# Two transformer blocks: the last output branch and the second output projection with the second 128 tokens behind the first, the second norm through a diagonal, and the router by halves of the tokens

## The chip, the cores and the metric

The kernel runs on 1 core of one Trainium2 chip, in one launch. The metric is the device time in microseconds (us) of that core; three executions of the kernel before took 1136.58, 1136.77 and 1137.79 us.

## What is computed

256 tokens of width 1024 in f32 go through two blocks. The part that matters here is the end of the second block's mixer and the start of its expert stage:

```python
merged = jax.nn.sigmoid(gate_a) * (o_mla @ w_o_mla) + jax.nn.sigmoid(gate_b) * (o_fox @ w_o_fox)
x = x + gate_m * (merged @ w_out)
h = rms_norm_2(x, g_ffn_norm[l]) * (1.0 + scale_f) + shift_f
scores = jax.nn.sigmoid((xf @ w_router).astype(jnp.float32))     # xf is h, 256 x 1024; 64 experts
# top 4 of 8 groups, top 6 experts, gates; then per expert
hb = jax.nn.silu(xb @ w_exp_gate[e]) * (xb @ w_exp_up[e])
# ... @ w_exp_down[e], summed with the shared expert, and a last rms_norm
```

## The kernel before, in words

Every engine runs a list of instructions written out by hand, with semaphores between the lists. The tokens are two halves, m = 0 and m = 1, of 128 each.

**Projections.** A weight matrix comes in 1 MB loads into a ring of 6 slots (`ring`). A load is cut into "pieces" of two 128-row blocks of the contraction. ScalarE (ACT) writes a piece's rounded part into `hl` (6 places, `hi_of`), VectorE (DVE) writes the remainder into `rlo`, and TensorE (PE) does, for a piece and a half of the tokens, 6 matmuls of 512 columns into a PSUM bank. The activations are a pair in the same way: `L0` or `L1`, a rounded part by ACT (`rounded`) and a remainder by DVE (`completed`). `project` runs a block's pieces in steps. A step holds (piece s, m = 0) and (piece s - lag, m = 1); the table `BEHIND` names the blocks that share one run and their lag, all others have lag 0. A place in `hl` and a slot of `ring` are free only when both halves have used the piece (`both`), and the queue of SyncE (SP) waits for that before it issues the next load. Functions in `at` are called behind a step.

The blocks around the change, in order: `of0 of1` (the first output branch), `om0 om1` (the last, `w_o_mla`, 2 pieces each), `wp0 wp1` (the second output projection, `w_out`, 4 pieces each). Block x0 gives columns 0 to 511, x1 the others. Behind `om0` and `om1` DVE multiplies with the gate and adds (`branch`, semaphore `merged2`). `turn("mT2")` transposes the sum by 16 PE transposes in four groups; ACT and DVE make the pair in `L0`; `wp0` and `wp1` follow. Behind each of them DVE scales and adds to the residual `R` (semaphore `r2_set`), and ACT squares with a sum over the row (`sq2_a`).

**Second norm and router.** DVE and ACT make 1/root of each token; DVE scales m = 0 into `xp` and ACT m = 1; PE transposes `xp` (`turn("h3T")`, 16 transposes); DVE shifts and scales m = 0 into `ht3`, ACT m = 1. Then PE: router for both halves (16 matmuls of 64 columns, one bank, `taken` once), the shared expert's gate and up for m = 0 (16 matmuls of 256 columns), 16 transposes of `ht3` ("h3", banks 2, 3, 0, 1), gate for m = 1, the ranks (which need DVE's choice of experts, `sel_set`), up for m = 1, small transposes, and `gather(0)`, which starts the experts. A plain f32 matmul stands in the trace as two records.

**Experts.** 64 experts in 32 pairs, 3 MB of weights each, through 15 slots of 1 MB (`slots_all`). SP issues a load as soon as PE has used what was in the slot. Six slots are the ring's, some others hold buffers of the projections: nine loads wait for the end of `wp` or for what comes behind it.

**mod.** The modulation vector is summed on GpSimd; `mod_sum(11)` is the last PE step of it (a 512-column matmul of `macc` with ones), which stands between `wp0` and `wp1`.

## Time and profile before

| | |
|---|---|
| runs | 1136.58, 1136.77, 1137.79 us (median 1136.77) |
| profiled execution, its own time | 1138.23 us |
| its span | 1136.5 us, so 1.7 us lie around it |
| PE busy | 1066.9 us (94%) |
| last branch starts on PE | 553.14 us |
| second projection ends on PE | 594.64 us |
| first gather of the experts | 636.53 us |
| last write of a result | about 1136 us |

Times in rows are us from the span's start, durations of a group are for all its instructions, and "idle before" is how long the engine had nothing in work ahead of the row, with what released it. PEld is PE's loading of the stationary operand, which goes beside its matmuls. The granted clock is 1.00 at 2.4 GHz and 0.50 at 1.2 GHz.

### The profile page before, as it was taken

How to read it: one execution, taken by the hardware profiler on the slowest of the kernel's cores; microseconds unless marked ns; L12 is line 12 of the kernel's file. 1: busy time of each engine (PE TensorE's matmuls, PEld its weight loads, DVE VectorE, ACT ScalarE, POOL GpSimd, SP SyncE). 2: the span in 40 equal slices, each digit the busy share in tenths (PEclk: the TensorE clock that was granted, in tenths of full speed). 3: DMA queues.
4: the chain of work that ended last, by engine and by line, in shares of the span. 5: the costliest groups of instructions: out<-in, count | busy, mean ns of one | idle time of the engine just before them, and what ended most of it. 6: DMA issues, size and time to landing. Idle time of an engine off the chain costs nothing. (4 is left out here: it accounts for less than half of the span.)

```text
span 1136.5 us, 12858 instructions
## 1 busy us (share of the span) xinstructions
PE 1066.9 (94%) x5006; PEld 708.3 (62%) x5006; DVE 552.4 (49%) x985; ACT 392.5 (35%) x677; POOL 339.2 (30%) x261
## 2 busy tenths in 40 slices
PE   6999999979999899899797999999999999999993
PEld 4887888868887788688576645353535444444442
DVE  5979766758657766764744312222222221212214
ACT  4645665446424554564323101111211111111112
POOL 1059855596685007909700000000000000000000
PEclk9999999989999899799896999999999999999997
DMA  9656653856665545454439299999999999999991
GB/s 327 212 185 220 218 189 134 331 175 225 240 225 183 181 148 185 149 186 150 176 135 400 78 394 416 412 417 417 417 418 418 418 416 417 416 417 416 419 369 38
DMA packets 93933, 320.65 MB, mean 282 GB/s; under 512 B 6288, under 2 KB 7328, under 8 KB 76976
## 3 DMA queue, kind: packets, MB, share of 16 engines
q1 hardware_dynamic: 92832, 316.07, 72.7%
q0 software_dynamic: 752, 3.22, 0.8%
q8 instruction: 41, 0.67, 0.2%
q10 hardware_dynamic: 288, 0.52, 0.1%
q14 instruction: 20, 0.16, 0.0%
HBM read 318.74 MB, written 1.05 MB: 281 GB/s over the span
## 5 line engine op out<-in xcount | busy, mean ns | idle before, releaser
L802 PE MATMUL ps<-hl,L 128*128 128x512 f32 (+1 forms) x1216 | 388.7, 401 | 14.0 <-DVE rlo L1602 8.5
L802 PEld LDWEIGHTS ps<-hl,L 128*128 128x128 f32 x1216 | 231.7, 193 | 64.1 <-issue 15.8
L1602 DVE TENSOR_TENSOR rlo<-ring,hl 128x1024 fp32r<-128x1024 f32 (+1 forms) x154 | 211.5, 1393 | 112.9 <-ACT hl L1236 112.5
L802 PE MATMUL ps<-rlo,L 128*128 128x512 f32 (+1 forms) x608 | 241.5, 397 | 0.0
L802 PE MATMUL ps<-slots_all,xe 128*64 128x512 f32 (+1 forms) x1056 | 226.9, 582 | 0.8 <-DVE rt L2385 0.8
L1236 ACT ACTIVATE hl<-ring 128x1024 fp32r<-128x1024 f32 (+1 forms) x154 | 158.9, 1054 | 182.0 <-PE ps L802 75.2
L763 POOL TENSOR_SCALAR ring<-ring,st 128x512 f32<-128x512 f32 x84 | 176.1, 2097 | 0.0
L791 POOL CAST two<-ident 64x128 fp32r<-64x128 f32 x64 | 19.1, 298 | 488.6 <-PE ps L802 487.1
L802 PEld LDWEIGHTS ps<-slots_all,xe 128*64 128x64 f32 x1056 | 73.9, 137 | 131.7 <-issue 128.5
L802 PEld LDWEIGHTS ps<-rlo,L 128*128 128x128 f32 x608 | 117.1, 193 | 24.8
L765 POOL TENSOR_TENSOR macc<-macc,ring 128x512 f32<-128x512 f32 x84 | 116.7, 1390 | 7.0
L802 PE MATMUL ps<-slots_all,hh 128*64 128x512 f32 x512 | 116.2, 596 | 0.0
L1608 DVE SCALAR_TENSOR_TENSOR hh<-ps,gslot,hh 128x256 f32<-128x256 f32 x32 | 15.5, 483 | 190.9 <-ACT hh L1236 190.9
L1236 ACT ACTIVATE hh<-ps 128x256 f32<-128x256 f32 x64 | 24.7, 387 | 207.1 <-PE ps L802 196.4
L1236 ACT ACTIVATE yy<-ps 128x512 fp32r<-128x512 f32 x64 | 35.0, 595 | 171.0 <-PE ps L802 165.4
L761 POOL TENSOR_SCALAR macc<-ring,st 128x512 f32<-128x512 f32 x12 | 20.6, 1718 | 219.3 <-DMA ring<-in_w_mod 191.5
L802 PEld LDWEIGHTS ps<-slots_all,hh 128*64 128x64 f32 x512 | 37.3, 138 | 73.0 <-issue 66.3
L1602 DVE TENSOR_TENSOR yy<-ps,yy 128x512 fp32r<-128x512 f32 x64 | 41.3, 686 | 58.8 <-ACT yy L1236 58.8
L802 PE MATMUL ps<-yy,ppt 128*128 128x512 f32 x256 | 65.2, 397 | 3.5 <-DVE yy L1602 3.5
L802 PE MATMUL ps<-pp,h3hl 128*128 128x512 f32 x256 | 59.7, 390 | 1.0 <-DVE rgt L1602 1.0
L1605 DVE TENSOR_SCALAR ppt<-ps,cols 128x256 fp32r<-128x256 f32 x32 | 15.5, 483 | 88.6 <-PE ps L802 88.6
L802 PEld LDWEIGHTS ps<-yy,ppt 128*128 128x128 f32 x256 | 48.2, 189 | 15.0 <-DVE yy L1602 4.5
(213 smaller groups left out, 915.9 us busy)
## 6 DMA issues: line engine op xcount, KB each, us to landing
slots_all<-in_w_exp_gate SPq DMA_DIRECT2D x64, 1024.0 KB, 19.9
slots_all<-in_w_exp_up SPq DMA_DIRECT2D x64, 1024.0 KB, 15.9
slots_all<-in_w_exp_down SPq DMA_DIRECT2D x64, 1024.0 KB, 16.7
ring<-in_w_in SPq DMA_DIRECT2D x49, 1024.0 KB, 5.4
ring<-in_w_mod SPq DMA_DIRECT2D x24, 1024.0 KB, 6.2
ring<-in_w_out SPq DMA_DIRECT2D x8, 1024.0 KB, 5.2
ring<-in_w_ple_gate SPq DMA_DIRECT2D x4, 1024.0 KB, 5.1
ring<-in_w_branch_a SPq DMA_DIRECT2D x4, 1024.0 KB, 7.2
```

The source lines that it names most:

```text
L761: e.tensor_scalar(acc, v, s, None, ALU.mult).then_inc(mac, 1)
L763: e.tensor_scalar(v, v, s, None, ALU.mult).then_inc(mac, 1)
L765: e.tensor_tensor(acc, acc, v, ALU.add).then_inc(mac, 1)
L791: x = e.tensor_copy(two[s, i % 2, :].rearrange("p (e c) -> p e c", e=2), spread(ident[s, 64 * r + 2 * i:64 * r + 2 * i + 2], 64))
L802: return e.matmul(o, l, r, start=start, stop=stop)
L1236: return e.activation(o, i, f, **kw)
L1602: return e.tensor_tensor(o, a, b, op)
L1605: return e.tensor_scalar(o, a, s1, s2, op0, op1) if op1 is not None else e.tensor_scalar(o, a, s1, None, op0)
L1608: return e.scalar_tensor_tensor(out=o, in0=a, scalar=s, in1=b, op0=op0, op1=op1)
```

## The change

It does these things:

1. `om0 om1` become one run with lag 3 (4 pieces, 7 steps), `wp0 wp1` one with lag 4 (8 pieces, 12 steps). The transposes of the merged sum go by halves: m = 0 behind step 4 of the first run, m = 1 behind step 1 of the second. DVE's branch and residual steps and ACT's squares are placed by half and column.
2. The scaled copy `xp` is gone. DVE writes the token's 1/root into a diagonal (`DIAG2`), and PE multiplies `R` with it (`h3_turn`, 8 plain f32 matmuls of 128 columns for each half, whose stationary operand is read with a stride of 8 elements), which transposes and scales at once. DVE shifts the first four of eight blocks of both halves, ACT the last four.
3. `mod_sum(11)` stands behind the first half's diagonal matmuls.
4. The router's matmuls go by halves, with the second half's diagonal matmuls and a part of the shared expert between them; ACT loads the table of the sigmoid ahead of its shifts; banks are given by hand, those of "h3" being 4 to 7.

```diff
+        def DIAG2(m):
+            return B(4)[:, m, 0:128]
...
-        BEHIND = (("bb0 bb1", 4), ("wo0 wo1", 4), ("c0", 4),)
+        BEHIND = (("bb0 bb1", 4), ("wo0 wo1", 4), ("c0", 4), ("om0 om1", 3), ("wp0 wp1", 4))
...
-        SUM_AT = {}
+        SUM_AT = {11: "end"}
...
-        AFTER = {"v0": "qT", "za0": "kT", "gb1": "yaT", "ba0": "ybT", "om1": "mT2"}
+        AFTER = {"v0": "qT", "za0": "kT", "gb1": "yaT", "ba0": "ybT"}
...
-        aux_turn_x("h3T", "va")
-        aux_x("router", "a")
...
+        aux(("h3T", 0, 0), "v", 0), aux(("h3T", 0, 4), "a", 2)
+        for c in MOD_SUM["end"]:
+            aux(("mod", c), "v", 4)
+        aux(("h3T", 1, 0), "v", 1), aux(("h3T", 1, 4), "a", 3)
+        aux("router", "a", 0)
+        aux(("sh", 0), "v", 2)
+        for n, (j0, m) in enumerate((j0, m) for j0 in (0, 4) for m in range(2)):
+            aux(("h3", m, j0), "v", 4 + n)
...
-            for name in ("om0", "om1"):
-                project(name, L1, l_ready("omT"))
-            turn("mT2", lambda m, j: GB2[:, m, 128 * j:128 * j + 128],
-                 lambda m, j0: w.wait_ge(merged2, 2 * (j0 // 4) + m + 1))
-            for name in ("wp0", "wp1"):
-                project(name, L0, l_ready("mT2"))
-            for c in MOD_SUM.get("end", ()):
-                mod_sum(c)
-
-
-            w.wait_ge(*evacuated("wp1", 1))
-            for name in aux_names[aux_dense - 4:aux_dense]:
-                w.wait_ge(*read(name))
-
-            def xp_ready(m, j0):
-                w.wait_ge(*((xp_v, 1) if m == 0 else (xp_a, 1)))
-
-            turn("h3T", lambda m, j: xp[:, m, 128 * j:128 * j + 128], xp_ready)
-            wait_turned("h3T")
-            b = take("router")
-            w.wait_ge(*here2("router"))
+            def merged_turn2(m):
+                turn_tokens("mT2", m, lambda m, j: GB2[:, m, 128 * j:128 * j + 128],
+                            lambda m, j0: w.wait_ge(merged2, 2 * m + j0 // 4 + 1))
+
+            project("om0", L1, l_ready("omT"), {4: lambda: merged_turn2(0)})
+            project("wp0", L0, l_ready("mT2"), {1: lambda: merged_turn2(1)})
...
+            def h3_turn(m):
+                w.wait_ge(*evacuated("wp0", m))
+                w.wait_ge(*evacuated("wp1", m))
+                spread_tokens("h3T", m, lambda m, j: R[:, m, :].rearrange("p (f k) -> p k f", k=8)[:, j, :], DIAG2,
+                              lambda m, j0: w.wait_ge(xp_set, m + 1))
+
+            def route(b, m):
+                w.wait_ge(*here2("router"))
+                for k in range(8):
+                    wait_read(("h3T", m, 4 * (k // 4)))
+                    x = mm(b[:, 64 * m:64 * m + 64], ht3[:, k, tok(m)], wr[:, k, :], k == 0, k == 7)
+                return x
...
-            b = take(("sh", 0))
-            shared_half(b, 0, "sg", wsg, 0)
-            taken(shared_half(b, 0, "su", wsu, 256))
+            h3_turn(0)
+            for c in MOD_SUM["end"]:
+                mod_sum(c)
+            br = take("router")
+            route(br, 0)
+            h3_turn(1)
+            b0 = take(("sh", 0))
+            shared_half(b0, 0, "sg", wsg, 0)
+            taken(route(br, 1))
+            taken(shared_half(b0, 0, "su", wsu, 256))
...
+            project("om0", at={5: lambda: rounded("mT2", tokens=(0,))})
+
+            def square2(m, c):
+                w.wait_ge(r2_set, 2 * m + c + 1)
+                act(B(2)[:, m, half(c)], R[:, m, half(c)], ACT.Square,
+                    accum_out=st[:, 64 + 2 * m + c:65 + 2 * m + c]).then_inc(sq2_a, 1)
+
+            def square_root2(m):
                 w.wait_ge(rt2_v, m + 1)
                 act(st[:, 68 + m:69 + m], st[:, 68 + m:69 + m], ACT.Sqrt).then_inc(rt2_a, 1)
-            w.wait_ge(rt2_v, 3)
-            act(xp[:, 1, :].rearrange("p (k f) -> p f k", k=8), R[:, 1, :].rearrange("p (f k) -> p f k", k=8), ACT.Copy,
-                scale=st[:, 71:72]).then_inc(xp_a, 1)
-            w.wait_ge(xp_v, 1)
-            for j0 in (0, 4):
-                aux_done(("h3T", 1, j0))
-                for j in range(4):
-                    x = act(ht3[:, j0 + j, tok(1)], bank(("h3T", 1, j0))[:, 128 * j:128 * j + 128], ACT.Identity,
-                            scale=Af[:, j0 + j:j0 + j + 1], bias=modcol[:, 2, j0 + j:j0 + j + 1])
+
+            def h3_shift(m):
+                aux_done(("h3T", m, 4))
+                for j in range(4, 8):
+                    x = act(ht3[:, j, tok(m)], bank(("h3T", m, 4))[:, 128 * (j - 4):128 * (j - 4) + 128], ACT.Identity,
+                            scale=Af[:, j:j + 1], bias=modcol[:, 2, j:j + 1])
                 x.then_inc(aux_a.sem, 1)
+
+            def second_turned():
+                rounded("mT2", tokens=(1,))
+                act(st[:, 255:256], ones[:, 0:1], ACT.Sqrt)
+
+            project("wp0", at={2: second_turned, 3: lambda: square2(0, 0)})
+
+
+            square2(0, 1)
+            square_root2(0)
+            square2(1, 0)
+            square2(1, 1)
+            square_root2(1)
+            act(st[:, 255:256], ones[:, 0:1], ACT.Sigmoid)
+            h3_shift(0)
+            h3_shift(1)
...
+            project("om0", at={1: lambda: om(0, 0), 3: lambda: om(0, 1), 4: lambda: om(1, 0),
+                               5: lambda: completed("mT2", tokens=(0,))})
+            om(1, 1)
...
+            def diagonal2(m):
+                w.wait_ge(rt2_a, m + 1)
+                mine(e.reciprocal(st[:, 70 + m:71 + m], st[:, 68 + m:69 + m]))
+                wait_mine()
+                tsc(DIAG2(m), ident[:, :], st[:, 70 + m:71 + m], None, ALU.mult, None).then_inc(xp_set, 1)
...
-            root(0, rt2_v, rt2_a, mine)
-            wait_mine()
-            tsc(xp[:, 0, :].rearrange("p (k f) -> p f k", k=8), R[:, 0, :].rearrange("p (f k) -> p f k", k=8),
-                st[:, 70:71], None, ALU.mult, None).then_inc(xp_v, 1)
-            root(1, rt2_v, rt2_a, then3)
...
+            project("wp0", at={2: lambda: completed("mT2", tokens=(1,)), 3: lambda: wp(0, 0)})
+
+
+            wp(1, 0)
+            wp(0, 1)
+            w.wait_ge(sq2_a, 2)
+            mean_square(0, rt2_v)
+            diagonal2(0)
+            wp(1, 1)
+            h3_shift(0)
+            w.wait_ge(sq2_a, 4)
+            mean_square(1, rt2_v)
+            diagonal2(1)
+            for c in MOD_SUM["end"]:
                 mod_sum(c)
+            h3_shift(1)
...```

On PE, from the end of the second projection to the last transposes ahead of the gather (`bs` with `rbuf` is the diagonal with R). Before, then changed:

```order
L806 MATMUL ps0<-ident_49,xp_99 128x128 x4
L806 MATMUL ps1<-ident_49,xp_99 128x128 x4
L806 MATMUL ps2<-ident_49,xp_99 128x128 x4
L806 MATMUL ps3<-ident_49,xp_99 128x128 x4
L802 MATMUL ps0<-slots_all_97,ht3_85 128x64 x16
L802 MATMUL ps1<-slots_all_97,ht3_85 128x256 x16
L806 MATMUL ps2<-ident_49,ht3_85 128x128 x4
```

```order
L803 MATMUL ps0<-bs_70,rbuf_63 128x128 x4
L803 MATMUL ps2<-bs_70,rbuf_63 128x128 x4
L803 MATMUL ps4<-macc_79,ones_51 128x512
L803 MATMUL ps0<-slots_all_97,ht3_85 128x64 x8
L803 MATMUL ps1<-bs_70,rbuf_63 128x128 x4
L803 MATMUL ps3<-bs_70,rbuf_63 128x128 x4
L803 MATMUL ps2<-slots_all_97,ht3_85 128x256 x8
L803 MATMUL ps0<-slots_all_97,ht3_85 128x64 x8
L803 MATMUL ps2<-slots_all_97,ht3_85 128x256 x8
L807 MATMUL ps4<-ident_49,ht3_85 128x128 x4
```

The 16 router matmuls have become 8 and 8, and the second half's diagonal matmuls and 8 matmuls of the shared expert stand between them.

On DVE, through the run of `om0 om1` and the start of `wp0` (`ps0` to `ps3` are om0 m = 0, om0 m = 1, om1 m = 0, om1 m = 1; `rlo` is a weight piece's remainder, `L0` that of the transposed sum). Before, then changed:

```order
L1602 TENSOR_TENSOR bs_70<-ps1,bs_70 128x512
L1602 TENSOR_TENSOR bs_70<-bs_70 128x512
L1602 TENSOR_TENSOR rlo_67<-ring_65,hl_66 128x1024 x2
L1602 TENSOR_TENSOR bs_70<-ps2,bs_70 128x512
L1602 TENSOR_TENSOR bs_70<-bs_70 128x512
L1602 TENSOR_TENSOR bs_70<-ps3,bs_70 128x512
L1602 TENSOR_TENSOR bs_70<-bs_70 128x512
L1602 TENSOR_TENSOR L0_68<-ps6,L0_68 128x4x128
L1602 TENSOR_TENSOR L0_68<-ps7,L0_68 128x4x128
```

```order
L1615 TENSOR_TENSOR rlo_67<-ring_65,hl_66 128x1024
L1615 TENSOR_TENSOR bs_70<-ps1,bs_70 128x512
L1615 TENSOR_TENSOR bs_70<-bs_70 128x512
L1615 TENSOR_TENSOR rlo_67<-ring_65,hl_66 128x1024
L1615 TENSOR_TENSOR L0_68<-ps6,L0_68 128x4x128
L1615 TENSOR_TENSOR L0_68<-ps7,L0_68 128x4x128
L1615 TENSOR_TENSOR rlo_67<-ring_65,hl_66 128x1024
L1615 TENSOR_TENSOR bs_70<-ps3,bs_70 128x512
L1615 TENSOR_TENSOR bs_70<-bs_70 128x512
L1615 TENSOR_TENSOR rlo_67<-ring_65,hl_66 128x1024
L1615 TENSOR_TENSOR L0_68<-ps4,L0_68 128x4x128
L1615 TENSOR_TENSOR L0_68<-ps5,L0_68 128x4x128
```

The last branch step of the second half (`ps3`) now stands behind the remainders of the first half and behind one more weight piece, the fifth of `w_out`.

## Rows read from the trace of the kernel before

**Rows 1.** Waits of SP, 600 to 1100 us; its issues; the chain that ended last.

```profile
SPq L735 <- PE ps L802: 318.0, 57, 17.1
...
651.59 0.89 SPq L735 DMA_DIRECT2D slots_all<-in_w_exp_down  x2
...
1097.19 12.54 PE ps L802 x88
```

**Rows 2.** Timeline of PE, branch `om` and projection `wp`: start us, us.

```profile
553.14 1.04 PE L802 MATMUL ps<-hl,L 128*128 128x512 f32 x2
...
564.46 1.03 PE L806 MATMUL ps<-ident,bs 128*128 128x128 f32 x8
568.08 0.66 PE L806 MATMUL ps<-ident,bs 128*128 128x128 f32 x4 [2.59 <-DVE bs L1602]
...
570.10 1.05 PE L802 MATMUL ps<-hl,L 128*128 128x512 f32 x2
...
582.69 1.02 PE L802 MATMUL ps<-macc,ones 128*128 128x512 f32 x2
...
584.26 0.62 PE L802 MATMUL ps<-hl,L 128*128 128x512 f32 x2
...
593.80 0.62 PE L802 MATMUL ps<-hl,L 128*128 128x512 f32 x2
```

**Rows 3.** Stretches: start:end, length, busy us (instructions) by engine, PEclk, DMA share, GB/s.

```profile
570.00:575.00 5.00, 5.00 (x17) 3.89 (x16) 2.97 (x4) 3.26 (x5) 0.00 (x0) 0.66 0.01 5
```

**Rows 4.** ACT and DVE on weight pieces of `w_out`, and the page's DMA issues (last number: us to landing).

```profile
564.38 1.06 ACT L1236 ACTIVATE hl<-ring 128x1024 fp32r<-128x1024 f32 x1 [4.10 <-DMA ring<-in_w_out]
565.47 1.23 DVE L1602 TENSOR_TENSOR rlo<-ring,hl 128x1024 fp32r<-128x1024 f32 x1 [1.50 <-ACT hl L1236]
...
ring<-in_w_out SPq DMA_DIRECT2D x8, 1024.0 KB, 5.2
```

**Rows 5.** Timeline of DVE and ACT behind the projection.

```profile
594.68 0.69 DVE L1602 TENSOR_TENSOR bs<-ps,gbuf 128x512 f32<-128x512 f32 x1
596.26 0.63 ACT L1236 ACTIVATE bs<-rbuf 128x512 f32<-128x512 f32 x1 [0.77 <-DVE rbuf L1602]
600.40 1.37 DVE L1605 TENSOR_SCALAR ht<-ps,st,modcol 128x128 f32<-128x128 f32 x4 [0.63 <-PE ps L806]
603.11 3.15 ACT L1236 ACTIVATE ht<-ps,modcol,st 128x128 f32<-128x128 f32 x8 [1.27 <-PE ps L806]
606.28 1.28 ACT L1236 ACT_TABLE_LOAD   x1
```

**Rows 6.** Timeline from the router to the first gather, all engines.

```profile
606.67 16.21 PE L802 MATMUL ps<-slots_all,ht 128*128 128x64 f32 x64 [1.95 <-ACT ht L1236]
613.76 0.28 ACT L1236 ACTIVATE rt<-ps 128x128 f32<-128x128 f32 x1 [6.20 <-PE ps L802]
...
618.92 0.62 DVE L1602 TENSOR_TENSOR rt<-rt 128x128 f32<-128x128 f32 x2
...
622.72 1.91 PE L806 MATMUL ps<-ident,ht 128*128 128x128 f32 x16
...
625.33 3.72 PE L802 MATMUL ps<-slots_all,ht 128*128 128x256 f32 x16 [0.70 <-DVE h3hl L1602]
...
629.95 3.67 PE L802 MATMUL ps<-slots_all,ht 128*128 128x256 f32 x16
...
636.53 3.69 PE L802 MATMUL ps<-pp,h3hl 128*128 128x512 f32 x15 [1.05 <-DVE rgt L1602]
```

**Rows 7.** A stretch of the router, columns as in rows 3.

```profile
612.00:614.00 2.00, 2.00 (x10) 1.97 (x10) 0.00 (x0) 0.23 (x1) 0.00 (x0) 0.50 0.97 406
```

**Rows 8.** Weight loads and matmuls with small or strided operands: ns min/median/max, first and last start.

```profile
L802 PEld LDWEIGHTS ps<-bs,rbuf x16: 187/192/192, 385.2 to 386.8; 128*128 128x128 f32 x16
...
L802 PEld LDWEIGHTS ps<-ones,macc x16: 195/218/218, 343.0 to 344.7; 128*64 128x64 f32 x16
...
385.15 2.05 PE L802 MATMUL ps<-bs,rbuf 128*128 128x128 f32 x16 [0.59 <-DVE bs L1605]
```

More of the change, by code:

```diff
@@ L1174, in shared_down @@
             def shared_down():
-                wait_read(("sT", 0), ("sT", 1))
+                wait_turned("h3")
+                wait_read(("sT", 0), ("sT", 1), *aux_names[aux_dense - 4:aux_dense], *(("mod", c) for c in MOD_SUM["end"]))
                 w.wait_ge(*here2("sd"))
@@ L1505, in _ @@
             rounded("omT", (0,))
-            for name in ("om0", "om1"):
-                project(name)
-            rounded("mT2")
-            act(st[:, 255:256], ones[:, 0:1], ACT.Sqrt)
-            for c in range(2):
-                project(f"wp{c}")
-                for m in range(2):
-                    w.wait_ge(r2_set, 2 * c + m + 1)
-                    act(B(1)[:, m, half(c)], R[:, m, half(c)], ACT.Square,
-                        accum_out=st[:, 64 + 2 * m + c:65 + 2 * m + c]).then_inc(sq2_a, 1)
```

70 lines of the change are left out of this document (25 added, 45 removed).

## The prediction

> **What bounds the kernel now.** I read the page first: PE is busy for 94% of the span, so an idle or slow PE is what there is to win. The chain that ended last is PE almost alone from 671 to 1109.7 us [rows 1]: in the expert stage PE waits for no weights. SP there waits for PE, 318 us in 57 waits, since a slot is refilled when PE has used it, and the stream begins again at 651.6 with the first pair's slots [rows 1]. Both PE and the loads of this stage hang on the start of the first gather at 636.53 [rows 6]; what comes before moves the end of the kernel one to one, as long as the nine loads issued at the end of `wp` land first. So the question is how much earlier the gather starts.
>
> Ahead of it lie two stretches. **Stretch A** is 553.14 to 594.64, 41.5 us, from `om` to the end of `wp`. Between the two PE does 16 transposes and waits for DVE's last branch steps, from 564.46 to 570.10 [rows 2]. After that the granted clock is 0.66 over 5 us [rows 3], that is 3.4 us at 1.2 GHz. **Stretch B** is 594.64 to 636.53, 41.9 us: adds and squares, root, `xp`, transposes, shifts, and only at 606.67 the router [rows 5, 6], which runs at a granted clock of 0.50 [rows 7].
>
> **Stretch A, before.** Three matmuls of 512 columns take 0.68 us (14 triples from 584.26 to 593.80 [rows 2]), so a piece for half of the tokens takes 1.36. There are 24 of these: 32.6. The slow first ones cost 0.4, the turn 5.6, the slow clock behind it 1.7 (half of 3.4), `mod_sum(11)` 0.9 (two records and the slow one behind, 582.69 to 584.26 less 0.68 [rows 2]). Sum 41.2, measured 41.5.
>
> **Stretch A, changed.** The 32.6 and 0.4 stay. The transposes stay too, 8 in 1.03 us [rows 2], so 2.1, but other matmuls stand around them. The waits, counted from the start of `om` (t = 0):
> - m = 0 is done at 5.8, its branch step (0.69 + 0.69 [rows 5] and a gap, 1.4) at 7.3, its transposes start at 8.6, behind step 4: no wait. They end at 9.6, and PE does the last two pieces of m = 1 until 12.3.
> - DVE meanwhile does a piece's remainder (1.23 [rows 4]), `om0` m = 1, another remainder, then the first two remainders of L0. The third `w_out` piece needs step 4 (8.6), ACT 1.06, DVE 1.23, so L0's first group stands at 12.9. PE waits 0.6.
> - The fifth `w_out` piece is in a load that takes the slot of `om0`. Before, both halves had used `om0` after 4 piece-halves, now after 6, at 8.6. A load of `w_out` lands in 5.2 us [rows 4]; ACT before waited 4.10 us for this very one at 564.38 [rows 4]. So it lands at 13.9, is rounded at 15.0 and its remainder done at 16.2. The last branch step (`ps3`) is queued behind it on DVE: done at 17.6. PE has ended step 1 of `wp` at 15.7 and four of the transposes at 16.2, and waits 1.5 us.
> - The hl places of the seventh and eighth piece come free at steps 4 and 5 of the run; ACT and DVE need 2.5 us and each following step gives 2.7. Behind ACT's first square nothing is late. I cost this at nothing; if one of them slips by 1 us, PE waits 1 us.
>
> Sum 32.6 + 0.4 + 2.1 + 2.1 = 37.2 against 41.5: **4.3 us** earlier. Of these 0.9 are `mod_sum(11)`, which I count in B.
>
> **Stretch B, changed.** T is the end of `wp`. m = 0 is done 6.8 us ahead of T (five piece-halves), and its adds (1.4, and 1.4 of m = 1 between), square (0.63 [rows 5] and its sum), mean, root and diagonal take some 4.2. The diagonal is ready before T, hidden by matmuls of m = 1; without that cover it would cost those 4.2.
>
> The price of the diagonal matmuls is the open one. With R read in order, 16 records took 2.05 us [rows 8], 0.125 each; that is the lower end, 2.0 for a half. Here R is the stationary operand and is read with a stride of 8 elements. The one load with this stride takes 218 ns for 64 columns, where one in order takes 192 for 128 [rows 8]. If the excess goes with the columns, a record needs about 0.27 and a half of the tokens 4.3; that is the upper end. I take 4.3, since the strided row is the nearest one.
>
> The Trainium skill (SBUF — State Buffer, section "Door 1: The DMA port swizzle") says that f32 can be strided by up to four elements for free and that each access to a new 16-byte line pays. Eight elements are past that, so the rule speaks against this change and for the upper end: by it the gain of the next paragraph is 6.9, and if it did not hold it would be 9.8. No row shows a 128-column load with this stride.
>
> PE then: diagonal, half 0, 4.3; `mod_sum(11)` 1.0; router half 0, first four blocks, 1.0 (16 records at 0.125 are 2.0; DVE's shift, 1.37 [rows 5], is done at T + 3.6). The last four blocks wait for ACT. ACT's list is: last square (T + 2.4), root of m = 1 (its mean is behind DVE's shift, so T + 4.2), the table load of 1.28 [rows 5] and a dummy, T + 5.7, then four shifts (half of 3.15 [rows 5]), T + 7.3. PE waits 1.0. Then router 1.0; diagonal, half 1, 4.3; gate of m = 0 3.65 (8 matmuls, 3.72 and 3.67 [rows 6]); router half 1 2.0; up 3.65; 16 transposes 1.9 [rows 6]; gate of m = 1 3.65; ranks 1.0 (625.33 + 3.65 to 629.95 [rows 6]); up 3.65; and as before 2.9 from there to the gather (633.6 to 636.53). Sum 35.0. DVE's choice of experts takes 5.8 from the router (613.76 to 619.54 [rows 6]) and is hidden by 9.2 us of PE; the second half's shifts (1.6) by the gate's 3.65. Against 41.9: **6.9 us** earlier.
>
> The Trainium skill (ScalarE: Activation LUTs, section "What ACT_TABLE_LOAD costs") adds a drain of 1.38 us to each load, 2.66 in all. Here the load takes 1.28 and the rows do not show what came before it; with 2.66 the wait of 1.0 would be 2.4 and the gain 1.4 smaller.
>
> **The clock.** The sums hold at 2.4 GHz. In the trace it fell behind the turn of stretch A [rows 3] and in the wait of stretch B, where the router did not bring it back [rows 7]. In the changed kernel both places have less idle time, but B has 12 us of matmuls with few columns and a wait. I take one fall, at the price of stretch A's, 1.7 us. None would be 0; one in each stretch, the second through the gate of m = 0, 1.7 + 3.0.
>
> **Sum.** 4.3 + 6.9 - 1.7 = 9.5, so the profiled execution of 1138.23 becomes 1128.7. The median of the runs, 1136.77, is 1.5 below it, and becomes **1127.3 us**.
>
> **The rivals.**
> 1. *Stride costs nothing.* A half takes 2.0, so 4.6 less of PE work; the wait for ACT grows by 1.7 (its last shift then stands at T + 6.7, where PE is at T + 4.0), so 2.9 net. With no fall of the clock: 4.3 + 6.9 + 2.9 = 14.1, 1122.7. For it: the strided loads followed each other at 0.12 us (343.0 to 344.7 for 16 [rows 8]), like those in order. Against it: 218 ns for half the columns. Chance 0.22.
> 2. *Clock and waits take half.* Falls in both stretches (4.7) and 2 us more of waits where DVE has its 14 steps between 5 and 19 us of A: 11.2 - 6.7 = 4.5, 1132.3. For it: both places had a fall before [rows 3, 7]. Against it: PE's idle time in A falls from 3.3 (5.6 less 2.3 of transposes) to 2.1. Chance 0.20.
> 3. *Diagonal matmuls dearer than the whole gain.* The 32 strided records stand alone on PE from T on, twice. Slower than before needs 11.2 us more, 0.27 + 11.2/32 = 0.62 us a record; at 0.75 the time would be 1136.8 + 32 x 0.48 - 11.2 = 1141.0. For it: no row has this load. Against it: the 64-column one is at 0.22. Chance 0.06.
> 4. *The end does not follow the gather.* If the expert loads were the bound, an earlier PE would wait for them at the end, 1136.8. Against it: the loads resume when PE frees slots [rows 1], so they move too. It is also the case in which the change does not do what it says. Chance 0.04.
>
> **How the numbers follow.** The forecast has 0.48. Its own range is 1125.5 to 1130 (a fall of the clock or none, the table load). The range for 8 in 10 takes in rival 1 (down to 1121.8 with a part of the idle time of A gone as well) and rival 2 (1133.5 with 1 us more). A measurement of this kernel can tell about 0.2%, 2.3 us: faster than that are forecast, rivals 1 and 2, 0.90; rival 4 is the same, 0.04; rival 3 slower, 0.06.
>
> **What would show it.** In the changed profile: `om` to the end of `wp` in some 37 us, with a wait for DVE `bs` of about 1.5 ahead of four transposes; diagonal matmuls beginning within 0.3 us of the end of `wp`, 16 records in 4.3 us (2.0 for rival 1, over 9 for rival 3); a wait of about 1 us in the router for ACT `ht`; the gather at about 627; the expert stage as long as before, 473 us from the gather to 1109.7. The prediction is wrong if the gather comes after 634, or if it comes early and PE then waits for a load.

## The result, and the profile after

The changed kernel takes **1122.97 us** (median of four runs, 1121.79 to 1124.01), the kernel before beside it 1136.67 (four runs, 1136.20 to 1137.79): a ratio of 0.988, 95% interval 0.9867 to 0.9893. That is 13.7 us less; 9.5 were forecast (1127.3, range 1121.8 to 1133.5). The sign, the place and the order of the gains were right; the gain was 4.2 us larger than forecast.

The profiled execution took 1123.09 us, with a span of 1121.3. PE is busy for 95% of it. First the timeline of PE in stretch A (as in [rows 2]: start us, us):

```profile
551.03 1.05 PE L803 MATMUL ps<-hl,L 128*128 128x512 f32 x2
...
559.67 1.03 PE L807 MATMUL ps<-ident,bs 128*128 128x128 f32 x8
...
564.10 0.70 PE L803 MATMUL ps<-hl,L 128*128 128x512 f32 x2 [0.63 <-DVE L L1615]
...
566.95 0.60 PE L807 MATMUL ps<-ident,bs 128*128 128x128 f32 x4
568.61 0.66 PE L807 MATMUL ps<-ident,bs 128*128 128x128 f32 x4 [1.06 <-DVE bs L1615]
569.02 0.71 PE L803 MATMUL ps<-hl,L 128*128 128x512 f32 x2
...
588.08 0.40 PE L803 MATMUL ps<-rlo,L 128*128 128x512 f32 x1
```

(`ps` is PSUM, and `bs` a buffer that holds the merged sum and, later, the diagonal.) `om` begins at 551.03 and `wp` ends at 588.48 (588.08 and 0.40): 37.4 us, where [rows 2] had 41.5. The transposes, which stood in one block, are in two, with matmuls between them. Where [rows 3] had a granted clock of 0.66, it is now 1.00. Windows of PE only (stretch, length, busy us with its instructions, PEclk, DMA share, GB/s):

```profile
550.00:555.00 5.00, 5.00 (x20) 0.89 0.00 0
570.00:575.00 5.00, 5.00 (x23) 1.00 0.01 2
...
592.00:597.00 5.00, 3.75 (x23) 1.00 0.99 406
597.00:602.00 5.00, 5.00 (x23) 1.00 1.02 428
...
607.00:612.00 5.00, 5.00 (x33) 1.00 1.02 409
```

Stretch B, from 588.48 to the gather at 621.39, takes 32.9 us; before it took 41.9 [rows 5, 6]:

```profile
588.31 3.85 PE L803 MATMUL ps<-bs,rbuf 128*128 128x128 f32 x16
592.00 1.02 PE L803 MATMUL ps<-macc,ones 128*128 128x512 f32 x2
592.86 1.00 PE L803 MATMUL ps<-slots_all,ht 128*128 128x64 f32 x8
595.11 1.10 PE L803 MATMUL ps<-slots_all,ht 128*128 128x64 f32 x8 [1.25 <-ACT ht L1241]
596.05 4.02 PE L803 MATMUL ps<-bs,rbuf 128*128 128x128 f32 x16
599.91 8.86 PE L803 MATMUL ps<-slots_all,ht 128*128 128x256 f32 x48
608.61 1.91 PE L807 MATMUL ps<-ident,ht 128*128 128x128 f32 x16
...
621.39 7.55 PE L803 MATMUL ps<-pp,h3hl 128*128 128x512 f32 x32 [1.05 <-DVE rgt L1615]
```

The first diagonal matmul starts as `wp` ends: the norm of the first half is hidden. The router's first matmul comes 4.4 us behind the end of `wp`; before it came 12.0 behind ([rows 5] to [rows 6]). The router ran at a granted clock of 0.50 there [rows 7] and runs at 1.00 here. ScalarE shows what the wait of 1.25 is (answers to [rows 5]):

```profile
591.94 0.20 ACT L1241 ACTIVATE st<-st 128x1 f32<-128x1 f32 x1 [1.26 <-DVE st L1618]
592.16 1.28 ACT L1241 ACT_TABLE_LOAD   x1
593.46 0.20 ACT L1241 ACTIVATE st<-ones 128x1 f32<-128x1 f32 x1
593.57 1.49 ACT L1241 ACTIVATE ht<-ps,modcol,st 128x128 f32<-128x128 f32 x4
```

The shift that the router waits for stands behind the table load. In the expert stage nothing has changed but the time at which it starts. SP's issue and the chain that ended last, against [rows 1]:

```profile
636.46 0.89 SPq L736 DMA_DIRECT2D slots_all<-in_w_exp_down  x2
```

```profile
1082.04 12.54 PE ps L803 x88
```

Both are 15.1 us earlier, like the gather (636.53 to 621.39). Of these 15.1 us, 4.1 come from stretch A, 9.0 from B and 2.1 from ahead of `om`, which began at 553.14 before and at 551.03 now behind code that is the same. The unchanged kernels traced again, below, show that such shifts come and go.

### The profile page after: what moved, and what is told of

Read it like the earlier page. It is cut to its first block and busy times, and to the rows that moved or that the text cites. A ratio compares the mean times of both kernels' runs of the same rounds, so it can differ in the third digit from the quotient of the medians.

```text
span 1121.3 us, 12888 instructions
## 1 busy us (share of the span) xinstructions
PE 1059.9 (95%) x5022; PEld 705.2 (63%) x5022; DVE 546.5 (49%) x986; ACT 390.3 (35%) x677; POOL 338.4 (30%) x261
## 3 DMA queue, kind: packets, MB, share of 16 engines
HBM read 318.74 MB, written 1.05 MB: 285 GB/s over the span
## 5 line engine op out<-in xcount | busy, mean ns | idle before, releaser
L803 PE MATMUL ps<-hl,L 128*128 128x512 f32 (+1 forms) x1216 | 388.3, 401 | 14.4 <-DVE rlo L1615 8.5
L803 PEld LDWEIGHTS ps<-hl,L 128*128 128x128 f32 x1216 | 231.5, 193 | 63.7 <-issue 15.7
L1615 DVE TENSOR_TENSOR rlo<-ring,hl 128x1024 fp32r<-128x1024 f32 (+1 forms) x154 | 206.2, 1359 | 113.7 <-ACT hl L1241 113.3
L803 PE MATMUL ps<-rlo,L 128*128 128x512 f32 (+1 forms) x608 | 241.1, 396 | 0.0
L803 PE MATMUL ps<-slots_all,xe 128*64 128x512 f32 (+1 forms) x1056 | 226.9, 582 | 0.8 <-DVE rt L2406 0.8
L1241 ACT ACTIVATE hl<-ring 128x1024 fp32r<-128x1024 f32 (+1 forms) x154 | 158.8, 1055 | 182.5 <-PE ps L803 73.3
L764 POOL TENSOR_SCALAR ring<-ring,st 128x512 f32<-128x512 f32 x84 | 171.0, 2036 | 0.0
L803 PEld LDWEIGHTS ps<-slots_all,xe 128*64 128x64 f32 x1056 | 73.9, 137 | 131.7 <-issue 128.5
L803 PEld LDWEIGHTS ps<-rlo,L 128*128 128x128 f32 x608 | 117.1, 193 | 24.9
L766 POOL TENSOR_TENSOR macc<-macc,ring 128x512 f32<-128x512 f32 x84 | 120.1, 1430 | 7.0
L803 PE MATMUL ps<-slots_all,hh 128*64 128x512 f32 x512 | 115.7, 594 | 0.0
L1241 ACT ACTIVATE hh<-ps 128x256 f32<-128x256 f32 x64 | 24.7, 386 | 207.4 <-PE ps L803 196.7
L1241 ACT ACTIVATE yy<-ps 128x512 fp32r<-128x512 f32 x64 | 35.0, 595 | 170.7 <-PE ps L803 170.7
L803 PEld LDWEIGHTS ps<-slots_all,hh 128*64 128x64 f32 x512 | 37.2, 138 | 72.5 <-issue 65.9
L1615 DVE TENSOR_TENSOR yy<-ps,yy 128x512 fp32r<-128x512 f32 x64 | 41.3, 686 | 58.5 <-ACT yy L1241 58.5
L803 PE MATMUL ps<-yy,ppt 128*128 128x512 f32 x256 | 65.6, 399 | 3.5 <-DVE yy L1615 3.5
L803 PE MATMUL ps<-pp,h3hl 128*128 128x512 f32 x256 | 59.7, 390 | 1.1 <-DVE rgt L1615 1.1
L1618 DVE TENSOR_SCALAR ppt<-ps,cols 128x256 fp32r<-128x256 f32 x32 | 15.5, 484 | 88.6 <-PE ps L803 88.6
L803 PEld LDWEIGHTS ps<-yy,ppt 128*128 128x128 f32 x256 | 48.6, 191 | 15.1 <-DVE yy L1615 4.5
## 6 DMA issues: line engine op xcount, KB each, us to landing
slots_all<-in_w_exp_gate SPq DMA_DIRECT2D x64, 1024.0 KB, 19.8
slots_all<-in_w_exp_up SPq DMA_DIRECT2D x64, 1024.0 KB, 15.8
slots_all<-in_w_exp_down SPq DMA_DIRECT2D x64, 1024.0 KB, 16.6
ring<-in_w_in SPq DMA_DIRECT2D x49, 1024.0 KB, 5.5
ring<-in_w_mod SPq DMA_DIRECT2D x24, 1024.0 KB, 5.2
ring<-in_w_out SPq DMA_DIRECT2D x8, 1024.0 KB, 5.1
ring<-in_w_ple_gate SPq DMA_DIRECT2D x4, 1024.0 KB, 5.1
ring<-in_w_branch_a SPq DMA_DIRECT2D x4, 1024.0 KB, 6.6
```

Source lines behind the costliest of these rows:

```text
L764: e.tensor_scalar(v, v, s, None, ALU.mult).then_inc(mac, 1)
L766: e.tensor_tensor(acc, acc, v, ALU.add).then_inc(mac, 1)
L803: return e.matmul(o, l, r, start=start, stop=stop)
L1241: return e.activation(o, i, f, **kw)
L1615: return e.tensor_tensor(o, a, b, op)
L1618: return e.tensor_scalar(o, a, s1, s2, op0, op1) if op1 is not None else e.tensor_scalar(o, a, s1, None, op0)
```

## The experiments

A single kernel's runs spread by up to 6.7 us (`xp`), and the traced run need not be near the median: that of `first` was its slowest (1126.36), that of `p4` its fastest (1119.78). So single edits are read in the trace: by the length of A (start of `om` to end of `wp`), of B (to the gather), and of the rest (gather to the end of the span).

The column "before beside it" is the median of the kernel before, run in the same session.

| kernel | A | B | rest | median, us | before beside it | ratio, 95% interval |
|---|---|---|---|---|---|---|
| before | 41.5 | 41.9 | 500.0 | 1136.67 | | |
| before, again | 42.0 | 41.2 | 499.9 | 1136.58 | 1136.82 | 0.9997, 0.9987 to 1.0008 |
| changed | 37.4 | 32.9 | 499.9 | 1122.97 | 1136.67 | 0.988, 0.9867 to 0.9893 |
| changed, again | 38.9 | 33.2 | 498.4 | 1123.62 | 1136.82 | 0.9885, 0.9868 to 0.9901 |
| stride1 | 38.8 | 30.5 | 500.1 | 1123.98 | 1136.74 | 0.9887, 0.9875 to 0.99 |
| table | 38.8 | 31.6 | 501.6 | 1125.41 | 1136.74 | 0.9899, 0.9885 to 0.9914 |
| first | 43.3 | 31.5 | 498.4 | 1123.53 | 1136.74 | 0.9878, 0.9863 to 0.9892 |
| xp | 39.0 | 32.0 | 498.4 | 1125.64 | 1136.74 | 0.9899, 0.9883 to 0.9916 |
| uom | 43.6 | 32.9 | 500.0 | 1128.65 | 1135.74 | 0.9937, 0.992 to 0.9953 |
| uwp | 41.8 | 35.5 | 500.0 | 1130.71 | 1135.74 | 0.9967, 0.9953 to 0.9981 |
| warm (on before) | 42.0 | 35.6 | 501.6 | 1132.27 | 1135.74 | 0.9968, 0.9958 to 0.9978 |
| p4 | 36.2 | 33.2 | 498.3 | 1122.23 | 1135.74 | 0.9895, 0.9876 to 0.9913 |
| late_before (on before) | 37.9 | 41.5 | 500.0 | 1132.48 | 1137.88 | 0.9955, 0.9939 to 0.997 |
| mixed_p4 | 37.7 | 28.6 | 500.0 | 1120.76 | 1136.82 | 0.986, 0.9845 to 0.9876 |

**What varies by itself.** The two kernels were traced again.

> The changed kernel, unchanged, for a second trace. Theory, its terms that hang on waits and instruction counts come again (waits of 0.63 and 1.06 to 1.5 in the stretch of om and wp, 1.25 in the router, diagonal 3.7 and 3.9, last stretch 32.9), and what differs is where the clock is half: the start of om costs 1.3 more where it is, and the expert stage takes 498.4, 499.9 or 501.6 from the gather to the end, in steps of about 1.6. Median 1122 to 1124. Rival, the last stretch too has a fall of the clock in some executions, so 34 to 36.

> The kernel before, unchanged, for a second trace of it. Theory, the clock falls in the head of its last stretch in every execution, because TensorE idles there through the adds, squares, root and scaling: from the end of wp to the gather 41 to 42 us again, with the router at a granted clock of 0.50. The stretch of om and wp again has a fall behind its turn: 41 to 43. Rival, the fall at the router is one of those that come and go between executions, like the one at the start of om (absent in the changed kernel's first trace, there in four of its variants): last stretch 36 to 38.

The changed kernel's waits came again: 0.64 and 1.14 in A, 1.25 in the router. The start of `om` ran at a granted clock of 0.56 (550 to 555), which made A 1.5 longer. B had a small fall of the clock (0.88 and 0.78 over 595 to 605) worth 0.3. The rest differed by 1.5. In the kernel before, both falls came again (0.66 over 565 to 570, then 0.59, 0.50, 0.50, 0.70 from 595 to 615). So the low clock at the router belongs to that kernel, and the theory holds. The one at the start of `om` is no part of the change: the same kernel had it at 0.89 in one trace and at 0.56 in the other. In the second trace of the kernel before, `om` began at 548.88, 4.3 us earlier than in the first.

**Is the clock part of the gain?** In `warm` the kernel before got ten idle matmuls in stretch B, five of them behind `wp`, two and three around the transposes:

```
+            def warm(n):
+                for _ in range(n):
+                    mm(PS[7][:, :], ident[:, :], GATES[:, 0, half(0)], True, True)
...
+            warm(5)
```

> The kernel before, with ten idle f32 matmuls of 512 columns into an unused bank in the stretch behind wp: five after its last piece, two after the first four transposes and three after the last, where TensorE waits anyway. In the kernel before the granted clock was 0.50 from about 597.6 to 618.0. Theory, part of the gain of the change in this stretch (41.9 to 32.9, where 7 was forecast at full clock) is that the clock no longer falls: at half clock the 32 router matmuls took 7.05 instead of 4.0, the 16 of gate and up 9.0 instead of 7.3, the transposes 1.3 more. With TensorE kept busy the stretch takes 36 to 38 us instead of 41.9 and the time is 1131 to 1133. Rival, the low clock there costs nothing that counts, because VectorE's and ScalarE's steps set the pace, or the idle matmuls delay the real ones by as much as they save: stretch 41 to 43, time 1136 to 1138.

B fell from 41.9 and 41.2 to 35.6 (36 to 38 were expected), and the time by 3.5 us (in the trace 1.6 of it was given back behind the gather, rest 501.6). The router and what follows ran at full clock; the 64 matmuls of [rows 6] took 10.69 instead of 16.21 and 15.67:

```profile
602.90 2.74 PE L802 MATMUL ps<-gbuf,ident 128*128 128x512 f32 x6
605.47 10.69 PE L802 MATMUL ps<-slots_all,ht 128*128 128x64 f32 x64
```

The theory holds. About 6 of the 9 us that the change gains in B are the clock, which the idle head of B had pulled down and the small matmuls behind it had not brought back. Work of no use brings these 6 without any of the change. The rest, 35.6 to 32.9, is got by subtraction: it is what the lag, the diagonal and the router by halves bring together at full clock.

**The stride of the diagonal matmuls.** `stride1` reads R in order, which puts the features in another order and gives other values, with the same instructions:

```
-spread_tokens("h3T", m, lambda m, j: R[:, m, :].rearrange("p (f k) -> p k f", k=8)[:, j, :], DIAG2,
+spread_tokens("h3T", m, lambda m, j: R[:, m, 128 * j:128 * j + 128], DIAG2,
```

> The diagonal matmuls read 128 consecutive elements of R instead of every eighth (the features reach the expert stage in another order, so the values differ, but every instruction stays). Theory, the stride costs TensorE time: in the changed kernel a load of 128 columns with the stride took 313 to 336 ns and eight records with it 3.69 and 3.86 us, where loads in order take 192. Then eight records take about 2.0 us, TensorE's work falls by 1.7 to 1.85 per half, about 3.5 together. The first half's part is given back as a longer wait for ScalarE's half of the columns, since that is held up by the table load and the shift and not by TensorE; so the gather comes 1.8 to 2.2 us earlier and the time is 1120.9 (1120.6 to 1121.4). Rival, the 3.7 us is the price of f32 matmuls of 128 columns whatever the layout: eight records still take 3.7, loads over 300 ns, time 1123.0.

Weight loads of the changed kernel, then those of `stride1` (ns min/median/max, first and last start):

```profile
L803 PEld LDWEIGHTS ps<-bs,rbuf x32: 313/335/336, 588.1 to 599.5; 128*128 128x128 f32 x32
```

```profile
L803 PEld LDWEIGHTS ps<-bs,rbuf x32: 188/192/192, 590.6 to 599.7; 128*128 128x128 f32 x32
```

The 16 records take 1.78 us instead of 3.69: 0.11 each against 0.23. The stride doubles their spacing. As expected, the first half's saving went partly into the wait for ScalarE, 1.25 to 2.29, and B fell by 2.5 (1.8 to 2.2 were expected). The median does not show it (1123.98): A began at half clock, and 2.5 us is inside the spread of the runs. The mechanism is settled by the rows, not by the time.

**The wait in the router.** `table` leaves the small Sigmoid out; `first` puts the second diagonal ahead of the router:

```
-            act(st[:, 255:256], ones[:, 0:1], ACT.Sigmoid)
             h3_shift(0)
```

```
+            h3_turn(1)
             br = take("router")
             route(br, 0)
-            h3_turn(1)
```

> The small Sigmoid ahead of the first half's shift is left out, so the table load (1.28 us) is made by the router's Sigmoid instead. Theory, the wait of 1.25 us in the router matmuls for ScalarE's first half is the table load: that wait falls to 0.1 or nothing, the shift starts at the end of the first half's diagonal matmuls, and the load lies beside the second half's matmuls or the choice of experts, where ScalarE is ahead of TensorE: time 1121.8 (1121.5 to 1122.2). Rival, the load lengthens the chain from the router's scores through the choice of experts to the gather, which ends within 1.05 us of wait at the gather's start: what is gained ahead of the router is lost there, time 1123.0 or up to 0.3 more.

> The second half's diagonal matmuls stand ahead of the first half's router matmuls. Theory, TensorE's wait of 1.25 us for ScalarE's columns is filled by work that waits for nothing (the second half's diagonal was ready about 3.2 us before its use, at 592.7 against a start at 592.9, so 0 to 0.2 of it is waited for): time 1121.8 (1121.6 to 1122.2). Rival, the scores of the second half still come at the same place behind ScalarE's second shift, now waited for in turn, or the choice of experts is what the gather waits for, so the wait only moves: time 1122.8 to 1123.0.

PE in `table`, then in `first`:

```profile
594.61 2.00 PE L803 MATMUL ps<-slots_all,ht 128*128 128x64 f32 x16
596.45 4.02 PE L803 MATMUL ps<-bs,rbuf 128*128 128x128 f32 x16
```

```profile
572.12 1.12 PE L807 MATMUL ps<-ident,bs 128*128 128x128 f32 x4 [2.94 <-DVE bs L1615]
...
599.13 4.00 PE L803 MATMUL ps<-bs,rbuf 128*128 128x128 f32 x16
602.97 10.65 PE L803 MATMUL ps<-slots_all,ht 128*128 128x64 f32 x64
```

In both, the wait is gone and B is 1.4 shorter. `table` shows that the load was the wait, and both show that the choice of experts did not become the bound. In `table` the load runs at 602.03, in idle time of ScalarE. The medians say nothing of it. In the trace of `table` the gain came back behind the gather, where the clock fell (the 32 matmuls that start there took 9.15 us instead of 7.55): its rest is 1.7 longer. All four runs of `table` lie between 1125.1 and 1125.5, so this may belong to it; whether it does stays open. In `first`, A was 43.3 for another reason, which the row shows: a wait of 2.94 for DVE `bs`, to which the next point comes.

**The diagonal against the scaled copy.** `xp` scales R on VectorE into `xp` again, by halves, and transposes it.

```
-tsc(DIAG2(m), ident[:, :], st[:, 70 + m:71 + m], None, ALU.mult, None)
+tsc(xp[:, m, :].rearrange("p (k f) -> p f k", k=8), R[:, m, :].rearrange("p (f k) -> p f k", k=8),
+    st[:, 70 + m:71 + m], None, ALU.mult, None)
...
```

> The diagonal is undone: VectorE scales the half of R by the root's reciprocal into a copy with the features regrouped, as in the kernel before but by halves of the tokens, and TensorE turns that with eight transposes. Theory, the diagonal is the dear way: a scaling on VectorE takes 1.3 us instead of 0.29 for a diagonal, while eight transposes take about 2.0 (16 took 4.12 with the clock granted in full) against 3.69 and 3.86. First half: +1.0 on VectorE ahead of TensorE and -1.7 on TensorE, so -0.7, of which the wait for the table load gives back some; second half: the scaling is hidden behind TensorE and -1.8 remains. Time 1120.8 (1120.2 to 1121.8). Rival, the diagonal pays as built, because the scaling stands ahead of the transposes on the path in both halves (+1.0 and +1.0) and the shift behind them is what the router waits for: time 1123 to 1125.

```profile
589.15 1.03 PE L807 MATMUL ps<-ident,xp 128*128 128x128 f32 x8
590.02 1.02 PE L803 MATMUL ps<-macc,ones 128*128 128x512 f32 x2
592.10 1.10 PE L803 MATMUL ps<-slots_all,ht 128*128 128x64 f32 x8 [1.05 <-DVE ht L1618]
595.50 1.97 PE L803 MATMUL ps<-slots_all,ht 128*128 128x64 f32 x8 [2.29 <-ACT ht L1241]
597.26 1.92 PE L807 MATMUL ps<-ident,xp 128*128 128x128 f32 x8
```

B is 32.0, 0.9 less than with the diagonal and not the 2.2 of the theory. The first half's transposes are 2.8 us shorter, and the waits behind them 2.1 longer. Behind these the clock fell again (0.88, 0.50 and 0.94 in the three stretches of 5 us from 590): eight router records took 1.97 instead of 1.10, and the second eight transposes 1.92 instead of 1.03. For the first half, with the lists of DVE and ACT as they stand, the dear diagonal is thus nearly free, since PE would wait in its place; for the second half, where PE waits for nothing, it costs its whole price, which `mixed_p4` shows below. The median, 1125.64, is over what this trace gives; its six runs lie at 1121.2 to 1121.4 (two, the traced one among them) and 1125.5 to 1127.9 (four). Why, is open.

**What the lags bring.** `uom` takes the lag from `om` alone, `uwp` from `wp` alone. Of each, the entry in the table of runs; the turns, squares and branch steps then follow by blocks of columns:

```
-        BEHIND = (("bb0 bb1", 4), ("wo0 wo1", 4), ("c0", 4), ("om0 om1", 3), ("wp0 wp1", 4))
+        BEHIND = (("bb0 bb1", 4), ("wo0 wo1", 4), ("c0", 4), ("wp0 wp1", 4))
```

> The lag is taken out of the last output branch alone: each piece of om0 and om1 is again multiplied for both halves of the tokens at once, and the first half is turned when the branch has ended; the second projection keeps its lag. Theory, the lag of this run hides VectorE's branch steps behind the other half's matmuls: without it TensorE waits again after the last piece, 3.5 us in the kernel before (5.6 from 564.46 to 570.10 less 2.1 of transposes) against 0.63 and 1.06 in the changed kernel, so the stretch from om to the end of wp is 1 to 2 us longer (38.8 was measured where the clock is half at its start, so 39.8 to 40.8), and 1.7 more if the clock falls behind the wait. The stretch from there to the gather stays at 32.9. Time 1124.5 to 1126.5. Rival, the waits of this stretch come from the late w_out piece and its load and not from the order of the halves: the stretch keeps its length within 0.5 us, time 1123 to 1124.

> The lag is taken out of the second output projection alone: both halves of the tokens end within 0.7 us of each other, so the first half's adds, squares, root and diagonal have no matmuls of the second half to hide them. Theory, the cover is worth what lies between a half's last matmul and its diagonal, 4.2 us: TensorE waits 4 to 5 us between the end of wp and the first diagonal matmul, and the stretch from the end of wp to the gather grows from 32.9 to 37 or 38; if the clock falls in that wait and the small matmuls behind it don't bring it back, up to 3 more. The stretch of om and wp changes by -0.5 to +1.5 (the second half is turned ahead of wp instead of one step into it). Time 1127 to 1131. Rival, most of the gain in this stretch is the diagonal and the router by halves, not the lag: growth under 2 us, time 1123 to 1125.

In `uom`, A is 43.6, more than the 39.8 to 40.8 expected (42.5 with a fall of the clock) and than the 41.5 before: waits of 2.93 and 1.19, and a fall of the clock (0.75 and 0.57 from 565 to 575). In `uwp`, A is 41.8 and B 35.5:

```profile
568.41 1.09 PE L806 MATMUL ps<-ident,bs 128*128 128x128 f32 x4 [5.04 <-DVE bs L1617]
...
594.30 4.15 PE L802 MATMUL ps<-bs,rbuf 128*128 128x128 f32 x16 [2.13 <-DVE bs L1620]
```

The cover of the first half's norm is worth 2.1, half of the 4.2 that I gave it. Without the lag the first half still ends 1.35 us ahead of the second, and its chain from DVE's first step at 590.84 to the diagonal's end at 594.15 is 3.3. The clock fell behind this wait (0.66 over 595 to 600), at a price of 0.4: from the first diagonal matmul to the router's first it is 4.95 us, against 4.55 in the changed kernel. Set beside `warm`, whose B of 35.6 has the old order at full clock, the 35.5 of `uwp` says something more: without the lag, the diagonal and the router by halves make B only about half a us shorter than the old order at full clock. Most of what they do bring without it is that the clock stays up (1.00 from 590 to the gather but for that one stretch, where the kernel before had 0.50 to 0.76 over 595 to 620). The larger part of the loss is in A, where the wait of 5.04 stands and neither theory had it; that the median lies in the expected range is luck. Both runs pointed to one thing: each long wait of A ends with DVE's branch steps, and DVE does them behind a weight piece that comes late. In `uwp`:

```profile
565.72 1.22 DVE L1617 TENSOR_TENSOR rlo<-ring,hl 128x1024 fp32r<-128x1024 f32 x1 [1.71 <-ACT hl L1242]
566.86 0.68 DVE L1617 TENSOR_TENSOR bs<-ps,bs 128x512 f32<-128x512 f32 x1
```

**The late piece.** In `p4`, on the changed kernel, the pieces of `wp1` are prepared only from `wp`'s first step on; `late_before` is the same edit on the kernel before:

```
-while at_piece < npieces and (at_piece < NH or used[at_piece - NH] < t) and all(
+while at_piece < npieces and (at_piece < blocks["wp1"][0] or t >= steps_of["wp0"][0][0]) and (
+        at_piece < NH or used[at_piece - NH] < t) and all(
```

> On the changed kernel: the pieces of wp1 are not prepared before wp's first step, so that VectorE does its last branch step before the remainder of the fifth w_out piece, whose load lands late. Theory, the wait for DVE bs ahead of the second half's last four transposes (1.06 in the changed kernel, 1.14 to 2.94 in its variants) is the wait for that load, passed on by VectorE's order: it falls to 0 to 0.2, and nothing else waits because the piece is needed only at step 4. Stretch om to end of wp 36.4 with the clock in full at its start, 37.7 where it is half there. Time 1122.0. Rival, the load itself is late for the step that uses the piece, so the wait moves to a matmul of wp1: stretch unchanged, time 1123.0.

> On the kernel before, with nothing of the change: the pieces of wp1 are not prepared before wp's first step, so VectorE does the four last branch steps ahead of the remainder of the piece whose load lands late. Theory, TensorE's waits of 2.59 and 0.76 us at the turn before wp are that load, passed on by VectorE's order (ScalarE rounds the piece 5.2 us after its load is issued in both kernels, and VectorE's branch steps stand behind it at 566.62, when om had ended at 564.5), and not the lack of other work to put there. The steps then start at about 564.0, the waits shrink to 0 to 0.2 and 0.6, the turn takes 3.2 us instead of 5.6, and with no long wait the clock does not fall behind it (1.7): from om to the end of wp 37.4 to 39.3 instead of 41.5 and 42.0, which is most of what the lag brought there; the last stretch stays at 41 to 42; time 1132.7 to 1134.5. Rival, the wait is there because both halves end together: it stays above 1.5 us, and the clock falls: stretch 40.5 to 42, time 1136 to 1137.

The first of the last branch steps on DVE, in the kernel before and then in `late_before`, with PE of `late_before` below, against [rows 2, 4]:

```profile
566.62 0.68 DVE L1602 TENSOR_TENSOR bs<-ps,bs 128x512 f32<-128x512 f32 x1
```

```profile
563.11 0.69 DVE L1603 TENSOR_TENSOR bs<-ps,bs 128x512 f32<-128x512 f32 x1 [0.25 <-PE ps L803]
...
565.81 2.48 DVE L1603 TENSOR_TENSOR L<-ps,L 128x512 fp32r<-128x512 f32 x4
```

```profile
564.27 1.47 PE L807 MATMUL ps<-ident,bs 128*128 128x128 f32 x12
566.04 0.63 PE L807 MATMUL ps<-ident,bs 128*128 128x128 f32 x4 [0.29 <-DVE bs L1603]
```

One condition in the planner, with no lag at all, brings A from 41.5 and 42.0 to 37.9, as the lag did (37.4 and 38.9): the waits of 2.59 and 0.76 shrink to 0.29, and the clock stays at 1.00. B is as before, 41.5. The time falls by 5.4 us (ratio 0.9955), of which the traces show 3.6 to 4.1 in A; the rest is within what the kernel before varies by (its medians beside the runs go from 1135.74 to 1137.88). In `p4` the wait for DVE `bs` is gone and A is 36.2, as expected. So in stretch A most of what the change brought was the cover of a badly placed wait, and could be had by placing it better; where its cover was thinner (`uom`, `uwp`), the wait was longer than before the change.

The landing of this load also explains the long A of `first`. ScalarE rounds the piece when it has landed, here in the changed kernel and in `first`:

```profile
564.91 2.01 ACT L1241 ACTIVATE hl<-ring 128x1024 fp32r<-128x1024 f32 x2 [3.00 <-DMA ring<-in_w_out]
```

```profile
568.42 2.00 ACT L1241 ACTIVATE hl<-ring 128x1024 fp32r<-128x1024 f32 x2 [4.88 <-DMA ring<-in_w_out]
```

The issues were at 559.87 and 561.50, so 5.0 and 6.9 us, and PE waited 1.06 and 2.94: the load's 1.9 us more went straight to PE.

**All together.** `mixed_p4` has p4's condition and table's edit, and scales and transposes the second half only:

```
+                if m == 0:
                     spread_tokens("h3T", m, lambda m, j: R[:, m, :].rearrange("p (f k) -> p k f", k=8)[:, j, :], DIAG2,
...
+                else:
+                    turn_tokens("h3T", m, lambda m, j: xp[:, m, 128 * j:128 * j + 128],
+                                lambda m, j0: w.wait_ge(xp_set, m + 1))
```

> The changed kernel with three edits together: VectorE does its last branch step before the late w_out piece (as in the run p4); the table load is left to the router's Sigmoid (as in table); and the second half alone is scaled by VectorE and transposed, while the first keeps its diagonal. Theory, the three act in different places, so they add up: the wait for DVE bs goes (-1.1), the router's wait goes (-1.25), and the second half's eight transposes take 1.0 instead of 3.9 for its diagonal matmuls, with the scaling (1.3 on VectorE) hidden behind the first half's router (-2.8): om to the end of wp 36.2 with the clock full at its start, then 28.8 to 29.2 to the gather; time 1123.0 less 4 to 5, 1118.0 to 1119.5. Rival, the choice of experts becomes the bound: VectorE's chain from the router's last matmul to the gather is 15 us long and what TensorE has beside it is no longer enough, so the last stretch ends at 30 to 31 and the time is 1120.5 to 1121.5.

```profile
590.81 3.85 PE L804 MATMUL ps<-bs,rbuf 128*128 128x128 f32 x16
594.49 1.02 PE L804 MATMUL ps<-macc,ones 128*128 128x512 f32 x2
595.35 2.01 PE L804 MATMUL ps<-slots_all,ht 128*128 128x64 f32 x16
597.20 1.04 PE L808 MATMUL ps<-ident,xp 128*128 128x128 f32 x8
598.07 8.86 PE L804 MATMUL ps<-slots_all,ht 128*128 128x256 f32 x48
```

B is 28.6 us with no wait ahead of the router's end (28.8 to 29.2 were expected), and A 37.7 though `om` began at half clock. The second half's eight transposes take 0.9 from start to start where its diagonal took 3.9. The median of 1120.76 is 16.1 us under the kernel before and 2.9 under the changed kernel beside it (1123.62), not the 4 to 5 forecast. In the traces the two stretches give 5.8; 1.9 are lost ahead of `om` and 1.6 behind the gather, in code that is the same, which leaves the 2.3 by which the spans differ (1121.9 and 1119.6). The intervals of the two ratios overlap, so by time alone it is only probably the fastest; by its stages it is.

## Why the prediction was right, and where it was off

**The bound.** Right. The gather sets the end: it came 15.1 us earlier, and so did the chain that ended last; from the gather to 1094.58 it is 473.2 us, 473 were forecast. Rival 4 is out.

**Stretch A.** 37.2 forecast, 37.4 measured; waits of 0.6 and 1.5 forecast, 0.63 and 1.06 measured; the fifth piece landing 13.9 us behind the start of `om`, measured 13.9 (564.91 less 551.03). The late load was named rightly. What I missed is that the same load, by the same order on DVE, made the wait of 2.59 before [rows 2, 4]: I booked the whole gain to the lag. `late_before` corrects this: 37.9 with no lag. So the length of the changed stretch was forecast rightly, and what made the gain was not.

**Stretch B.** 35.0 forecast, 32.9 measured. Piece by piece, from one start to the next:

| piece | forecast | measured |
|---|---|---|
| diagonal, half 0, from the end of `wp` | 4.3 | 3.5 |
| `mod_sum(11)` | 1.0 | 0.9 |
| router half 0, wait in it | 2.0, 1.0 | 1.9, 1.25 |
| diagonal, half 1 | 4.3 | 3.9 |
| gate, router half 1, up | 9.3 | 8.7 |
| transposes | 1.9 | 1.7 |
| gate, ranks, up of m = 1 | 8.3 | 8.0 |
| from there to the gather | 2.9 | 3.0 |

The diagonal was mis-sized: 0.23 to 0.24 us a record instead of 0.27. Most of the smaller differences have one source: I added the lengths of groups, and a group's length runs on past the start of the next by some 0.16 us (3.85 against the 3.69 from 588.31 to 592.00). The term "router, last four blocks wait for ACT" was right in place and size, and so was its cause, the table load. Between the activation before the load, which ends at 592.14, and the one behind it, which starts at 593.46, there is the load alone, from 592.16 to 593.44. The Trainium skill (ScalarE: Activation LUTs, section "What ACT_TABLE_LOAD costs") adds a drain of 1.38 us to a load; the trace has none. The prediction says that the rows do not show what came before the load, but [rows 5] do: the shifts end at 606.26 (603.11 and 3.15) and the load starts at 606.28, so no drain stood there either. A weight load with a stride of eight elements takes 335 ns, one in order 192. In this the trace agrees with the Trainium skill (SBUF — State Buffer, section "Door 1: The DMA port swizzle"), by which an f32 access can be strided by four elements for free and pays beyond.

**The clock.** This was the term that failed. I booked one fall as a loss, 1.7 us; there was none in either stretch. Together with the 2.1 us of B, less the 0.2 of A, this makes the difference in the profile: 13.0 in A and B where 9.5 were forecast. I had also counted the recovered clock without saying so: the 35.0 was summed at 2.4 GHz against a 41.9 of which 6 were the low clock, as `warm` shows. I should have split B's gain into 6 of clock and 1 of order; then it would have been plain how much of the gain hung on the clock.

**The rivals.** Rival 1 named nearly the time that came (1122.7), by a wrong mechanism: the stride is not free. Its second half, no fall of the clock, was right in this trace. Rival 2's larger falls came in variants with long waits (`uom`, `first`, `uwp`, `xp`). But small ones came in B with waits no longer than in the first trace (1.25): in the changed kernel's second trace, and in `p4`, where A and B are otherwise as expected:

```profile
595.00:600.00 5.00, 5.00 (x22) 0.66 1.02 428
```

Each of the two cost about 0.3, so a fall in B is a matter of the execution too, and the 0 of the first trace is not a sure term. Rival 3 is out at 0.23 us a record. Of the signs under "what would show it" two did not come: 3.7 instead of 4.3 for the 16 records, and the gather at 621.4 instead of 627. Of the latter's 5.6, 3.5 are explained above, and 2.1 are the earlier start of `om`.

## What to carry to other kernels

Before work is reordered to hide a wait, look at what the engine that is waited for has ahead in its queue. Here one weight piece with a late load stood before the last branch steps, and moving it was worth as much in that stretch as the whole reordering. The idle stretch with small matmuls behind it cost twice here, once idle and once in the clock; price the two apart, and try idle matmuls as a test of the second. A dear operation on an engine that would otherwise wait is nearly free, and the same operation a few us later costs its whole price, so the two halves of a symmetric piece of work may want different forms.
